# Hybrid decoder step, head loop: 64-column products ahead of the 32-column ones, sample queries on column tiles, three steps in another order

## What is computed

```python
o = einsum('bhts,bshv->bthv', att, v) + einsum('bthk,bhkv->bthv', q * exp(b), S)
S_new = exp(b_last)[..., None] * S + einsum('bshk,bshv->bhkv', k_dec, v)
oa = oa * rsqrt(mean(oa * oa, axis=-1) + EPS) * a_gnorm
ha = oa * silu(za)
```

## Time and profile before

| | us |
|---|---|
| median of 3 runs (1317.21 to 1319.89) | 1318.37 |
| profiled execution, its own time | 1319.32 |
| its span, first to last instruction | 1317.5 |
| PE busy | 1288.1 (98%) |
| DVE / ACT / POOL busy | 594.5 / 518.2 / 259.9 |
| mean granted PE clock | 0.992 |

### The profile page before, as it was taken

How to read it: one execution, slowest core, us unless ns; L and a number is a source line. 1 busy time by engine, 2 the same in 40 slices (tenths; PEclk the granted TensorE clock), 3 DMA queues, 4 the chain that set the end, 5 groups by cost and what they waited for, 6 DMA issues and landing times.

```text
span 1317.5 us, 23139 instructions
## 1 busy us (share of the span) xinstructions
PE 1288.1 (98%) x9148; PEld 1230.1 (93%) x9148; DVE 594.5 (45%) x1238; ACT 518.2 (39%) x1018; POOL 259.9 (20%) x119
## 2 busy tenths in 40 slices
PE   5999999999999999999999999999999999999998
PEld 5999999999999999999999999999999899999885
DVE  5655656564747474520000066656555202345132
ACT  6553544444453535431111255555555324114111
POOL 1122221212223222122222211111111121342000
PEclk9999999999999999999999999999999999999999
DMA  6212121202020202111111311111110212241330
GB/s 198 67 35 64 36 64 34 80 18 80 18 80 18 80 23 75 50 49 48 48 48 41 96 42 25 31 32 32 32 32 11 82 32 65 63 97 32 119 125 36
DMA packets 136753, 73.63 MB, mean 56 GB/s; under 512 B 37185, under 2 KB 133138, under 8 KB 136690
## 3 DMA queue, kind: packets, MB, share of 16 engines
q1 hardware_dynamic: 136706, 72.99, 20.1%
HBM read 63.77 MB, written 10.22 MB: 56 GB/s over the span
## 4 chain that ended last, share of the span: by engine, by line
PE 57%; ACT 0%; DVE 0%; issue 0%; ACTq 0%
PE pj L983 39%; PE pj L999 3%; PE pj L1340 3%; PE ps_a L1340 1%; PE ps_e L1340 1%; PE ps_a L1199 1%; PE ps_e L1237 1%; PE ps_d L1237 1%; PE ps_c L1199 1%; PE ps_d L1340 1%; PE ps_b L1340 1%; PE ps_c L1340 1%; PE ps_c L1224 1%; PE ps_b L1224 1%; PE ps_a L1224 0%; PE ps_e L1224 0%
## 5 line engine op out<-in xcount | busy, mean ns | idle before, releaser
L983 PE MATMUL pj<-xn_h,w_h 128*128 128x352 f32 x1656 | 544.4, 329 | 3.4 <-POOL w_l L571 2.0
L983 PE MATMUL pj<-xn_h,w_l 128*128 128x352 f32 x1656 | 535.4, 323 | 0.0
L983 PE MATMUL pj<-xn_l,w_h 128*128 128x352 f32 x1656 | 534.7, 323 | 0.0
L571 POOL TENSOR_TENSOR w_l<-w_raw,w_h 128x1024 fp32r<-128x1024 f32 x82 | 202.2, 2466 | 673.4 <-ACT w_h L643 649.9
L983 PEld LDWEIGHTS pj<-xn_h,w_h 128*128 128x128 f32 x1656 | 313.5, 189 | 12.6 <-issue 5.2
L983 PEld LDWEIGHTS pj<-xn_l,w_h 128*128 128x128 f32 x1656 | 314.5, 190 | 0.1
L983 PEld LDWEIGHTS pj<-xn_h,w_l 128*128 128x128 f32 x1656 | 313.7, 189 | 0.0
L643 ACT ACTIVATE w_h<-w_raw 128x1024 fp32r<-128x1024 f32 x81 | 85.4, 1055 | 113.7 <-PE pj L983 99.8
L1584 DVE TENSOR_TENSOR mg<-sg,pj 128x352 f32 (+1 forms) x24 | 12.4, 521 | 151.9 <-PE pj L983 150.4
L856 ACT ACTIVATE scores<-scores,stat 128x256 f32<-128x256 f32 (+1 forms) x128 | 61.5, 484 | 0.0
L983 PE MATMUL pj<-hl_l,w_h 128*128 128x352 f32 x168 | 54.2, 323 | 0.0
(11 more groups left out here) (401 smaller groups left out, 2132.9 us busy)
## 6 DMA issues: line engine op xcount, KB each, us to landing
w_raw<-in_w_in_dram SPq DMA_DIRECT2D x132, 256.0 KB, 3.4
x_t<-in_x_prompt_dram SPq DMA_DIRECT2D x8, 512.0 KB, 8.0
s<-in_state_hgrn_dram SPq DMA_DIRECT2D x8, 512.0 KB, 4.2
out_dram<-s SPq DMA_DIRECT2D x8, 512.0 KB, 3.2
w_raw<-in_w_pa_dram SPq DMA_DIRECT2D x16, 256.0 KB, 3.0
w_raw<-in_w_pb_dram SPq DMA_DIRECT2D x16, 256.0 KB, 4.5
wo_raw<-in_w_out_dram SPq DMA_DIRECT2D x8, 512.0 KB, 3.9
x_o<-in_x_prompt_dram SPq DMA_DIRECT2D x8, 512.0 KB, 4.2
```

The lines of the kernel that those rows point to most:

```text
L571: g.tensor_tensor(w_l[p][:], w_raw[p][:], w_h[p][:].bitcast(F32), ALU.subtract).then_inc(w_lo_ready, 1)
L983: mm = nc.tensor.matmul(pj[g][:, 0:W], w[:, kt, :], x[:, kt, span(g)], start=(kt == 0 and m == 0), stop=(kt == KT - 1 and m == 2))
```

## The change

- **Small products:** the eight 64 x 64 products run first, then all 32 x 32 pieces chunk by chunk.
- **Sample queries:** a new step `sx` behind `ps` holds the 32 query columns of the samples as weights, in four 32-column tiles, and streams each of the eight states (128 columns) through one of them, two per tile. DVE clears two chunks of `k_tok` (`sx0`, inside the state chain) and copies from the result only what belongs to each sequence (`sxm`, a masked copy). `os` is then one product of masked scores and values, now over 128 partitions with zeroed rows, and two products that turn `k_tok` with a selecting matrix `sel`. `sel` and `own` come by eight more loads behind the masks'.
- **POOL:** the scaling of the states waits for `sx`, not for `os`.
- **Mean of squares:** one slot later on PE, and waiting for the last low half of the squares.
- **DVE:** query gate 1 ahead of the output gates; the state additions ahead of the low halves of the squares.
- **Prologue:** block 1 is rounded by DVE behind the third tile's low halves, no longer by ACT behind the fourth tile.

```diff
@@ -136,17 +136,16 @@
     products = ["kD", "m64q", "m64k", "m32q", "m32k", "dqm", "dkm", "qIm", "kt0", "kt1", "kts", "k3_hi", "k3_hi2", "k3_lo"]
-    chain = [f"s{c}" for c in range(1, NC + 1)]
-    masked = ["att0", "att1", "atts"]
-    gated_head = ["gate0", "gate1", "gates", "sl0", "sl1", "sls"]
+    chain = [f"s{c}" for c in range(1, 6)] + ["sx0"] + [f"s{c}" for c in range(6, NC + 1)]
+    masked = ["att0", "att1", "atts", "sxm"]
+    gated_head = ["gate0", "gate1", "gates", "so0", "so1", "sl0", "sl1", "sls"]
     merged = [f"{s}{n}" for n in range(2 * SLOTS) for s in "gm"]
         ("pro", ["par", "lbm", "lbd0", "lbd1", "lbs", "lbr", "lb", "oml", "noml", "mean"] + per_tile(["xn"], ["lo_a", "lo_b"])
-         + ["att0", "atts0", "reset", "reset_p", "reset_s", "q0", "q1"] + exponents[:2] + ["q2"] + exponents[2:8] + ["z0"] + exponents[8:12]
+         + ["att0", "atts0", "vts0", "reset", "reset_p", "reset_s", "q0", "q1"] + exponents[:2] + ["q2"] + exponents[2:8] + ["z0"] + exponents[8:12]
          + ["z1"] + exponents[12:] + ["z2"], 1, 0),
-        ("head", ["ha"] + products + chain + masked + exponents + ["q0"] + gated_head
-         + ["q1", "so0", "so1", "q2"] + each_slot("z"), HEADS - 1, 1),
-        ("last", ["ha"] + products + chain + masked + gated_head + ["so0", "so1"]
+        ("head", ["ha"] + products + chain + masked + exponents + ["q0", "q1"] + gated_head + ["q2"] + each_slot("z"), HEADS - 1, 1),
+        ("last", ["ha"] + products + chain + masked + gated_head
          + each_tile("l", 0, 5) + ["hal"] + each_tile("l", 5), 1, 0),
@@ -158,7 +157,7 @@
     ])
-    head_products = ["vt0", "vt1", "vts", "kt0", "kt1", "kts", "p0", "p1", "ps", "u0", "u1",
+    head_products = ["vt0", "vt1", "vts", "kt0", "kt1", "kts", "p0", "p1", "ps", "sx", "u0", "u1",
                      "o0", "o1", "os", "us0", "us1", "ms0", "ms1", "mss"]
@@ -244,7 +243,9 @@
         rs = qI
-        att_s = sb("att_s", [NS, NS], where=area)
+        att_s = sb("att_s", [P, NS], where=area)
+        sel = sb("sel", [P, NS], where=area)
+        own = sb("own", [P, NB // 4], where=area)
         reset = sb("reset", [P, T], mybir.dt.bfloat16, where=area)
@@ -426,6 +427,9 @@
             sp.dma_start(batch_m[:], c_batch).then_inc(masks_loaded, 16)
+            for n in range(4):
+                sp.dma_start(sel[NS * n:NS * (n + 1), :], c_ident[0:NS, 0:NS]).then_inc(masks_loaded, 16)
+                sp.dma_start(own[NS * n:NS * (n + 1), :], c_batch[0:NS, 2 * n:2 * n + 2]).then_inc(masks_loaded, 16)
@@ -580,7 +584,7 @@
                 if is_first(i):
-                    g.wait_ge(masks_loaded, 48)
+                    g.wait_ge(masks_loaded, 16 * 11)
                 g.wait_ge(act_done, act.at(now, "v3_hi2"))
@@ -590,7 +594,7 @@
-                g.wait_ge(pe_done, pe.at(now, "os"))
+                g.wait_ge(pe_done, pe.at(now, "sx"))
                 g.tensor_tensor(s0[:], s0[:], E[:, NC:NC + NB].rearrange("p (b o) -> p b o", o=1).to_broadcast([P, NB, P]),
@@ -665,8 +669,8 @@
                                      ACT.Copy).then_inc(act_done, act.tick(pr, f"hi_{s}{t}"))
-                    if t in (0, 3):
-                        split_hi(pro(t // 3))
+                    if t == 0:
+                        split_hi(pro(0))
@@ -1086,10 +1090,12 @@
                 t.wait_ge(dve_done, dve.at(now, "dkm"))
+                for c in range(NC):
+                    bank, o = (ps_a, ps_b)[c // 4], c % 4 * P
+                    nc.tensor.matmul(bank[0:64, o + 64:o + 128], d64[:, c, 0, :], d64[:, c, 1, :], start=True, stop=True)
                 for n, bank in enumerate((ps_a, ps_b)):
                         c, o = 4 * n + j, j * P
-                        nc.tensor.matmul(bank[0:64, o + 64:o + 128], d64[:, c, 0, :], d64[:, c, 1, :], start=True, stop=True)
                         for m in range(2):
@@ -1103,6 +1109,12 @@
                 nc.tensor.matmul(ps_e[0:NS, 256:256 + NS], dk[:, SEQ:T], dq[:, SEQ:T], start=True, stop=True).then_inc(pe_done, pe.tick(now, "ps"))
+                t.wait_ge(s0_loaded, i * 16 + 16)
+                t.wait_ge(dve_done, dve.at(now, "qIm"))
+                for m in range(NB):
+                    rows_m = slice(NS * (m // 2), NS * (m // 2 + 1))
+                    mm = nc.tensor.matmul(ps_e[rows_m, m % 2 * P:(m % 2 + 1) * P], qI[:, SEQ:T], s0[:, m, :], start=True, stop=True)
+                mm.then_inc(pe_done, pe.tick(now, "sx"))
                 for n, bank in enumerate((ps_c, ps_d)):
@@ -1111,8 +1123,7 @@
-                t.wait_ge(dve_done, dve.at(now, "atts"))
-                t.wait_ge(dve_done, dve.at(now, "qIm"))
+                t.wait_ge(dve_done, dve.at(now, "sxm"))
                 for n, bank in enumerate((ps_e, ps_c)):
@@ -1120,11 +1131,11 @@
                     mm.then_inc(pe_done, pe.tick(now, f"o{n}"))
-                t.wait_ge(s0_loaded, i * 16 + 16)
-                nc.tensor.matmul(ps_d[:, 0:NS], v_tok[0:NS, NC, :], att_s[:, :], start=True, stop=True)
-                for m in range(NB):
-                    e = SEQ + DEC * m
-                    mm = nc.tensor.matmul(ps_d[:, DEC * m:DEC * (m + 1)], s0[:, m, :], qI[:, e:e + DEC], start=False, stop=True, skip_group_check=True)
+                if is_first(i):
+                    t.wait_ge(masks_loaded, 16 * 11)
+                nc.tensor.matmul(ps_d[:, 0:NS], v_tok[:, NC, :], att_s[:, :], start=True, stop=False)
+                for r in range(NB // 4):
+                    mm = nc.tensor.matmul(ps_d[:, 0:NS], k_tok[:, r, :], sel[:, :], start=False, stop=(r == NB // 4 - 1))
                 mm.then_inc(pe_done, pe.tick(now, "os"))
@@ -1132,12 +1143,12 @@
                 gate_slot(3, "q", (dve_done, dve), 0)
-
-                t.wait_ge(dve_done, dve.at(now, "so1"))
+                gate_slot(3, "q", (dve_done, dve), 1)
+
+                t.wait_ge(dve_done, dve.at(now, "sls"))
                 for n, bank in (("0", ps_a[:, :]), ("1", ps_b[:, :]), ("s", ps_d[:, 64:64 + NS])):
                     nc.tensor.matmul(bank, mean_m[:, :], sq_l[:, part[n]], start=False, stop=True).then_inc(pe_done, pe.tick(now, f"ms{n}"))
-                gate_slot(3, "q", (dve_done, dve), 1)
                 gate_slot(3, "q", (dve_done, dve), 2)
@@ -1394,10 +1405,15 @@
                        ALU.subtract).then_inc(dve_done, dve.tick(pr, f"lo_{s}{t}"))
+                if t == 2:
+                    v.wait_ge(w_loaded[1], 32)
+                    v.wait_ge(w_hi_ready, 1)
+                    v.tensor_copy(w_h[1][:], w_raw[1][:]).then_inc(w_hi_ready, 1)
             v.memset(att_s[:], 0.0).then_inc(dve_done, dve.tick(pr, "atts0"))
+            v.memset(v_tok[:, NC, :], 0.0).then_inc(dve_done, dve.tick(pr, "vts0"))
@@ -1517,20 +1533,25 @@
                         continue
+                    if c == 5:
+                        v.memset(k_tok[:, 0:NB // 4, :], 0.0).then_inc(dve_done, done("sx0"))
                     need(dve, dve_done, f"s{c}")
                     if c == NC - 1:
-                        need(pe, pe_done, "ps")
+                        need(pe, pe_done, "sx")
                     if c == NC - 1 and not is_first(i):
                 if is_first(i):
-                    v.wait_ge(masks_loaded, 48)
+                    v.wait_ge(masks_loaded, 16 * 11)
                 for n, bank in enumerate((ps_a, ps_b)):
                                       bank[:].rearrange("p (c t) -> p c t", c=4)).then_inc(dve_done, done(f"att{n}"))
-                v.copy_predicated(att_s[:], causal_s[:], ps_e[0:NS, 256:256 + NS]).then_inc(dve_done, done("atts"))
+                v.copy_predicated(att_s[0:NS, :], causal_s[:], ps_e[0:NS, 256:256 + NS]).then_inc(dve_done, done("atts"))
+
+                v.copy_predicated(k_tok[:, 0:NB // 4, :], own[:].bitcast(I32).rearrange("p (r o) -> p r o", o=1).to_broadcast([P, NB // 4, P]),
+                                  ps_e[:, 0:NB // 4 * P].rearrange("p (r v) -> p r v", r=NB // 4)).then_inc(dve_done, done("sxm"))
@@ -1540,17 +1561,16 @@
                     gated(now, "q", 0, q)
+                    gated(now, "q", 1, q)
                 gate("gate0", "sh0", ps_e, half(0), slice(0, 512))
                 gate("gates", "shs", ps_d, slice(SEQ, T), slice(0, NS))
-                for n in "01s":
-                    tt(sq_l[:, part[n]], vT[:, part[n]], sq_h[:, part[n]].bitcast(F32), ALU.subtract).then_inc(dve_done, done(f"sl{n}"))
-                if not last:
-                    gated(now, "q", 1, q)
                 need(pool, pool_done, "s0e")
                     tt(s0[:, 4 * n:4 * n + 4, :], s0[:, 4 * n:4 * n + 4, :], bank[:].rearrange("p (b v) -> p b v", b=4), ALU.add).then_inc(dve_done, done(f"so{n}"))
+                for n in "01s":
+                    tt(sq_l[:, part[n]], vT[:, part[n]], sq_h[:, part[n]].bitcast(F32), ALU.subtract).then_inc(dve_done, done(f"sl{n}"))
                 if last:
                     need(dve, dve_done, "so1")
```

## The result

| | us |
|---|---|
| before, median of the runs beside it | 1317.88 |
| after, median of four runs | 1286.08 (1283.51, 1283.94, 1288.21, 1288.21) |
| ratio, 95% interval | 0.9749 [0.9733, 0.9766] |
| profiled execution of after, its own time / span | 1288.21 / 1286.4 |

The kernel is faster by 2.5% by that ratio (2.4% by the two medians). The forecast of 1285.3 lies 0.8 from the median.

The account below looks back on a forecast made before the run. TensorE, busy 98% of the span, was taken as the bound. Terms 13.6 + 8.7 + 2.0 + 6.3 + 3.9 - 1.4 = 33.1 us off the profiled 1319.32 give 1286.2, against the median 1285.3; range 1281 to 1298.

Parts of the forecast that it names:

- Small products: Head loop: 2 changes of tile shape for 16, twelve 32-column records a chunk as a 0.14 us burst; 13.6 us gained.
- Rival B: Small products: records limited by feeding, at 0.036 us each the reordering gains nothing; 1298.9 us, chance 0.17.
- Sample queries: Each head: six end records save 1.56 us, sixteen early ones in four parallel tiles cost 0.47; 8.7 us gained.
- Rival A: Early sample products: column tiles start in program order, 1.46 us in place of 0.47; 1293.2 us, chance 0.13.
- GpSimd's stall: Heads: earlier scaling of the states ends TensorE's wait for GpSimd's low halves; 2.0 us gained, at most 3.7.
- rival D: Heads 0 to 6: VectorE's exponents stand for GpSimd, query gate late; slower, 1327 us at 8 us a head, chance 0.03.
- The clock: Heads 0, 2, 4, 7: half-clock falls follow the 4-column records, never another stage, and go; 6.3 us gained.
- one of the prediction's own signs of being wrong: Heads: the prediction is wrong if the clock falls in another stage; no size given.
- The prologue: Rounding the second weight block on VectorE removes TensorE's 2.29 us wait and the half-clock stretch after it; 3.9 us gained.
- rival C: Prologue: GpSimd wins the tie with VectorE's next row tile, TensorE waits there, gain 0; 1289.2 us, chance 0.14.
- Last head: End of the last head: three low halves now follow the second state addition; 1.4 us lost, 0.5 to 2.
- Order on VectorE: Each head: about 0.7 us of added VectorE work fits, leaving 1.7 before the query gate; nothing gained or lost.

Follow-up runs that it names:

- x5: The kernel before with only the small products reordered, the eight 64-column products of a head first: 1304.3 us, ratio 0.9900.
- x6: x1 with the small products in their old order: 1299.8 us.
- x7: x1 with all sixteen early sample products in one column tile in place of four, so computed wrongly: 1295.6 us.
- x8: x1 with GpSimd's scaling of the states waiting for the last sample record again, as in the kernel before: 1297.8 us.
- x1: The changed kernel, but GpSimd begins the low half of the prologue's second block only when VectorE has normalised the fourth row tile: 1284.2 us.
- x2: The changed kernel, but VectorE normalises the prologue's fourth row tile only when GpSimd has finished the second block's low half: 1287.9 us.
- x9: The kernel before with the prologue's part of the change alone: 1314.1 us, ratio 0.9971.
- x4: x1 with the last head alone in its old order, squares' low halves ahead of the state additions: 1283.4 us.

## Why the prediction was right, point by point

- **Small products: 13.6 expected, 14.7.** The reading of the change of shape held. What x5 and x6 show is the price of the order; that it falls due at each change of shape is read from the spacing. The sixteen 64-column records and one change take 142.32 to 143.39, 1.07 (1.10 said). The 32-column records take 143.39 to 144.53, 1.14 with the change behind them (1.22 said): 0.13 a chunk for the 0.14 of the burst, so the term was low by hundredths times eight. Rival B falls with x5 and x6. The Trainium skill, "TensorE: Matmul & The Clock Gate", section "Wait — 56ns, not 53.3ns?", has starts no closer than about 25 ns; the trace differs, with 96 records in 1.04, 0.011 us apart, kept up for the whole stage.
- **Sample queries: 8.7 expected, 9.2.** The early sixteen cost 0.49 (0.47 said), the end 1.64 less (1.56 said). Rival A falls: in program order it would have been 1.46, and x7 shows what one tile alone costs. The Trainium skill, "TensorE: Matmul & The Clock Gate", section "The mechanism" of its Part 3, has matmuls start strictly in program order; the rows of 32-column tiles differ from it, by the starts in the earlier trace rows and by the 0.49 here, though the sixteen records share one line and their own order can't be read.
- **GpSimd's stall: 2.0 expected, 2.6** (bound 3.7). The step was right in size, but incomplete: it priced the earlier scaling by the stall of before. x8 shows that in the changed kernel the earlier scaling carries 13.5, since without it GpSimd would meet VectorE's exponents. The prediction had these facts in its rival D, and did not ask what the other parts would have done without this one. (At 8 us a head that rival comes to 1285.3 + 7 x (8 - 1.7) = 1329.4, not 1327.)
- **The clock: 6.3 expected, 5.0 net.** Right in the heads: in the eight profiles without the 4-column records the clock is 1.00 from the first head to the last head's mean of squares, with them it falls in four, eight and three of the eight heads, each time right behind them. No run has these records together with the rest of the change, so the link rests on where the falls stand. The step that failed is "never any other stage of a head": behind the last head's wait a new stretch appeared, one of the prediction's own signs of being wrong, and took 1.3. What sets that one is open.
- **The prologue: 3.9 expected, 0.4 here or about 4.5.** This is the term that missed, and not by its size. The prediction saw the tie and took VectorE as first, with rival C for the other case; by the times of x1 and x2 each is first in two of the four runs. With VectorE first the part held: counted from the first row tile on TensorE to the first head's products it is 73.12 before (10.78 to 83.90) and 68.57 in x1 (10.18 to 78.75), 4.55 less, and x9 measures 3.5 (2.4 to 5.1). With GpSimd first it is 72.41 (11.05 to 83.46), 0.7 less. So the forecast of 1285.3 belongs to neither group: it lies 1.6 above the one and 2.9 below the other. That the median, between two runs of each, comes out 0.8 from it is luck.
- **Last head: 1.4 lost expected, 1.3 by the wait, 1.0 by the path.** The wait grew from 1.21 to 2.52, for the three low halves (1.39). x4 shows that only 1.0 of it is on the path, that is, delays what TensorE does next, as ScalarE's gate is next.
- **Order on VectorE: nothing expected, nothing found.** No wait for VectorE stands ahead of a slot in heads 0 to 6. But VectorE does stand for GpSimd: the first exponent takes 1.91 in place of 0.81, 1.1 a head, which the prediction put at nothing. It went into the slack (the room before TensorE would wait), which was put at 1.7. In x8 the query gates start 25.77 behind the head's small products (139.42 to 165.19), in x1 23.07 (137.61 to 160.68): 2.7 later makes a wait of 1.6, so 1.1 is what x1 has left.

With the terms as measured on the path, 14.7 + 9.2 + 2.6 + 5.0 + 0.4 - 1.0 = 30.9; the spans differ by 31.1, and 0.2 is in no term.

## What to carry to other kernels

Group small matmuls by the shape of their array tile: fourteen changes of shape fewer saved 1.84 us a head here, about 0.1 us each, and no view names it as a wait. Let the larger operand stream through several column tiles rather than a few columns behind many loads; here the falls of the clock in the heads went with those records. Before a GpSimd operation is moved, list which VectorE operations it will lie beside, with and without the other parts of the change. Where two engines tie for the same memory, set the order by a wait, or each execution draws its own.

## What the runs showed of the hardware that was not expected

- Some VectorE operations that meet a running GpSimd one do not share with it but wait for its end, whatever their own size: 32 columns took 1.89 in place of 0.18, a row tile 3.41 in place of 1.28. Others pass: the low halves of line 1406, which read one operand from a PSUM bank, take their usual 0.68 beside GpSimd's 14.84 to 17.21 of the changed kernel:

```profile
15.89 0.68 DVE L1406 TENSOR_TENSOR xn_l<-ps_d,xn_h 128x512 fp32r<-128x512 f32 x1
```

  The Trainium skill, "SBUF — State Buffer", section "SBUF: two separate sides", states it as an exclusive lock held for the whole instruction, for a VectorE operation with two inputs in SBUF against a GpSimd one that reads SBUF, or one in a mode that uses both ports. These rows agree: the two that waited read two SBUF tiles. A 0.04 us lead at 18.44 cost about 4 at the first head.
- A fall of the clock can follow a thin stretch of work, but does not follow each one: 4 of 8, 8 of 8 and 3 of 8 heads for the same sixteen 4-column records, when only what stands ahead of them is moved.
